# Row selectors of two quads in four moved to GpSimd and ScalarE in the gate scatter of a two-block forward pass

## What is computed

```python
gate = jax.nn.softmax(best, axis=-1)
...
act = jax.nn.gelu(jnp.einsum('tkd,td->tk', u_emb[eb], tb), approximate=False) * gb
return jnp.einsum('tk,tkd->td', act, v_emb[eb])
```

## Time and profile before

| | |
|---|---|
| median of three runs | 1703.91 us |
| the profiled execution, its own time | 1701.01 us |
| its span, first to last instruction | 1699.2 us |
| gate scatter, first selector to last quad | about 920 to 1012 us of the span |
| loop pass of VectorE in the scatter (four quads) | 15 passes, from 927.3 to 1010.5 us |
| granted TensorE clock over the span | 0.99 of full speed |

### The profile page before, as it was taken

How to read it: one execution, slowest core, us unless ns; L and a number is a source line. 1 busy time by engine, 2 the same in 40 slices (tenths; PEclk the granted TensorE clock), 3 DMA queues, 4 the chain that set the end, 5 groups by cost and what they waited for, 6 DMA issues and landing times.

```text
span 1699.2 us, 32624 instructions
## 1 busy us (share of the span) xinstructions
PE 1648.2 (97%) x12606; PEld 1511.1 (89%) x12606; DVE 1174.3 (69%) x2143; ACT 802.4 (47%) x1223; POOL 100.3 (6%) x124
## 2 busy tenths in 40 slices
PE   8999999999999999989999989999999999999998
PEld 3999969999999998879898878999999999999997
DVE  4757746777745779547598998666666666666665
ACT  2524535566535574325214983444444444444444
POOL 0000000022200001200052000000000000000000
PEclk9999999999999999979999999999999999999999
DMA  8866414545554443204233015555555555455553
GB/s 333 311 239 234 165 48 149 189 176 187 179 180 148 149 150 124 77 3 170 103 125 124 26 51 195 178 196 177 193 182 188 190 180 197 175 196 179 191 184 125
DMA packets 38826, 278.94 MB, mean 164 GB/s; under 512 B 4432, under 2 KB 4560, under 8 KB 5328
## 3 DMA queue, kind: packets, MB, share of 16 engines
q1 hardware_dynamic: 35424, 254.82, 41.9%
q0 software_dynamic: 2304, 16.78, 2.6%
q10 hardware_dynamic: 1008, 6.05, 1.0%
HBM read 276.58 MB, written 1.05 MB: 163 GB/s over the span
## 4 chain that ended last, share of the span: by engine, by line
PE 86%; DVE 7%; ACT 4%; issue 2%; DMA 1%; DVEq 0%; POOL 0%; ACTq 0%; POOLq 0%
PE ps L460 86%; DVE piece L1718 2%; ACT piece L1208 1%; DMA ring<-in_stream 1%; DVE pconst_sb L2463 1%; DVE cols L2463 0%; DVE late L2463 0%; DVE arena L1768 0%; DMA small<-in_cT 0%; ACT arena L1247 0%; DVEq L2463 0%; DVE arena L1805 0%; ACT arena L1563 0%; ACT L1243 0%; DVE arena L1785 0%
## 5 line engine op out<-in xcount | busy, mean ns | idle before, releaser
L460 PEld LDWEIGHTS ps<-h_r,piece 128*128 128x128 f32 x5664 | 697.3, 192 | 21.0 <-issue 8.7
L460 PE MATMUL ps<-h_r,piece 128*128 128x256 f32 x5664 | 706.5, 284 | 5.8 <-DVE piece L1718 4.9
L1718 DVE TENSOR_TENSOR piece<-ring,piece 128x1024 fp32r<-128x1024 f32 x434 | 533.3, 1237 | 242.9 <-ACT piece L1208 241.5
L1208 ACT ACTIVATE piece<-ring 128x1024 fp32r<-128x1024 f32 x432 | 452.7, 1056 | 355.1 <-PE ps L460 348.4
L460 PE MATMUL ps<-piece,late_r 128*128 128x512 f32 x1536 | 370.1, 391 | 1.4 <-DVE late_r L2485 1.4
L460 PEld LDWEIGHTS ps<-piece,late_r 128*128 128x128 f32 x1536 | 281.1, 188 | 55.4 <-issue 1.8
L2480 DVE TENSOR_TENSOR late<-late,arena 128x256 f32<-128x256 f32 x113 | 72.1, 638 | 117.5 <-ACT late L1674 117.5
L1674 ACT ACTIVATE late<-ps 128x256 f32<-128x256 f32 x113 | 43.5, 385 | 200.5 <-PE ps L460 200.5
L460 PE MATMUL ps<-arena,ring 128*128 128x256 f32 x480 | 110.5, 379 | 1.6 <-DVE arena L1785 1.6
L460 PEld LDWEIGHTS ps<-arena,ring 128*128 128x128 f32 x480 | 88.1, 190 | 12.3 <-issue 2.0
L460 PE MATMUL ps<-arena 64*64 64x64 f32 (+7 forms) x930 | 90.1, 315 | 9.0 <-DVE arena L2246 3.5
(11 more groups left out here) (325 smaller groups left out, 1703.6 us busy)
## 6 DMA issues: line engine op xcount, KB each, us to landing
ring<-in_stream SPq DMA_DIRECT2D x240, 1024.0 KB, 4.8
arena<-in_mod POOLq DMA_DIRECT2D x16, 1024.0 KB, 6.4
arena<-in_const ACTq DMA_DIRECT2D x1, 2256.0 KB, 10.2
arena<-in_const ACTq DMA_DIRECT2D x1, 1648.0 KB, 9.4
xres<-in_xT SPq DMA_DIRECT2D x1, 1024.0 KB, 6.8
arena<-in_xT SPq DMA_DIRECT2D x1, 1024.0 KB, 7.6
arena<-in_subk ACTq DMA_DIRECT2D x1, 1024.0 KB, 4.9
out<-arena SPq DMA_DIRECT2D x4, 256.0 KB, 2.1
```

The source lines that it names most:

```text
L460: mm_last[0] = nc.tensor.matmul(*args, **kw)
L1208: A(piece[:, 0, c % 3], ring[:, p % RING, s], ACT.Copy).then_inc(S["hi_ready"], 1)
L1718: TT(piece[:, 1, c % 3], ring[:, p % RING, s], piece[:, 0, c % 3].bitcast(F32), ALU.subtract).then_inc(S["lo_ready"], 1)
```

## The change

GpSimd now makes (row - index)^2 for the quads with q mod 4 = 0 and 1: a broadcast subtract and a multiply of the tile by itself, 128x512 each, with a wait on its own semaphore between them. It does so for 32 quads, behind `number` and the two casts in its program. From q = 4 on the subtract waits for the matmuls of quad q - 4. ScalarE clamps these tiles with the same Relu (`rows_end`), and goes on making squares and Relu itself for q mod 4 = 3. VectorE keeps the compare for q mod 4 = 2 only. TensorE waits for `row_hot` in three quads of four. In ScalarE's order the Relu of quads 0 and 1 of each four stands ahead of the copy of quad q - 2. The semaphore `place_no` is renamed `pool_done` and goes on counting (it stands at 35 after `number`).

```diff
--- before.py
+++ after.py
@@ -422,11 +422,11 @@
                 for c in range(2):
                     g.tensor_tensor(e[:, 2 * c:2 * c + 2], e[:, 2 * c:2 * c + 2],
                                     topf[:, :, 2 * hh + c, :].unsqueeze(2).to_broadcast([P, 2, 16, 16]),
-                                    ALU.mult).then_inc(S["place_no"], 1)
+                                    ALU.mult).then_inc(S["pool_done"], 1)
                 steps = 5 * hh + 2
                 for m in (8, 4, 2):
-                    pool.wait_ge(S["place_no"], steps)
-                    g.tensor_tensor(e[:, :, :, 0:m], e[:, :, :, 0:m], e[:, :, :, m:2 * m], ALU.add).then_inc(S["place_no"], 1)
+                    pool.wait_ge(S["pool_done"], steps)
+                    g.tensor_tensor(e[:, :, :, 0:m], e[:, :, :, 0:m], e[:, :, :, m:2 * m], ALU.add).then_inc(S["pool_done"], 1)
                     steps += 1
 
             for hh in range(7):
@@ -439,6 +439,17 @@
                     pool.wait_ge(loaded[first % RING], 16 * (first // RING + 1))
                 pool.wait_ge(S["piece_used"], c - 1 - s)
                 g.tensor_copy(piece[:, 0, c % 3], ring[:, first % RING, s]).then_inc(S["hi_ready"], 1)
+
+            pool.wait_ge(S["selt_sb"], 2)
+            for n in range(L // 8):
+                q = 4 * (n // 2) + n % 2
+                r = row_hot[q % 4]
+                if q >= 4:
+                    pool.wait_ge(S["g_mm"], 2 * q - 6)
+                g.tensor_tensor(r, selT[:, 0, 4 * q:4 * q + 4].unsqueeze(2).to_broadcast([P, 4, P]),
+                                iota.unsqueeze(1).to_broadcast([P, 4, P]), ALU.subtract).then_inc(S["pool_done"], 1)
+                pool.wait_ge(S["pool_done"], 36 + 2 * n)
+                g.tensor_tensor(r, r, r, ALU.mult).then_inc(S["pool_done"], 1)
 
 
         @block.tensor
@@ -1113,8 +1124,8 @@
                 for b in range(2):
                     pe.wait_ge(S["oh_ready"], 2 * q + b + 1)
                     if b == 0:
-                        if q % 2 == 1:
-                            pe.wait_ge(S["row_hot"], q // 2 + 1)
+                        if q % 4 != 2:
+                            pe.wait_ge(S["row_hot"], 3 * (q // 4) + (1, 2, None, 3)[q % 4])
                         if q >= 3:
                             pe.wait_ge(S["g_sb"], q - 2)
                     for e in range(2):
@@ -1645,20 +1656,23 @@
 
             def rows_end(q):
 
-                act.wait_ge(S["row_square"], q // 2 + 1)
+                if q % 4 == 3:
+                    act.wait_ge(S["row_square"], q // 4 + 1)
+                else:
+                    act.wait_ge(S["pool_done"], 37 + 2 * (2 * (q // 4) + q % 4))
                 A(row_hot[q % 4], row_hot[q % 4], ACT.Relu, scale=-1.0, bias=1.0).then_inc(S["row_hot"], 1)
 
             act.wait_ge(S["selt_sb"], 2)
             late_e = CHOICE
             for q in range(L // 4):
-                if q % 2 == 1:
+                if q % 4 == 3:
                     rows(q)
-                if q >= 2 and q % 4 != 1:
+                if q % 4 < 2:
+                    rows_end(q)
+                if q >= 2:
                     gates_out(q - 2)
-                if q % 2 == 1:
+                if q % 4 == 3:
                     rows_end(q)
-                if q >= 2 and q % 4 == 1:
-                    gates_out(q - 2)
                 if late_e < EARLY - 1 and q == 13 + 14 * (late_e - CHOICE):
                     T = TURN["peer"] + late_e
                     act.wait_ge(S["acc_ready"], T + 1)
@@ -2364,7 +2378,7 @@
 
             def gather(hh):
 
-                dve.wait_ge(S["place_no"], 5 * hh + 5)
+                dve.wait_ge(S["pool_done"], 5 * hh + 5)
                 e = place_eq[hh % 2].rearrange("p (c t) k j -> p c t k j", c=2)
                 TT(selv[:, :, 0:2, 16 * hh:16 * hh + 16].rearrange("p t c k -> p c t k"), e[:, :, :, :, 0], e[:, :, :, :, 1],
                    ALU.add).then_inc(S["placed"], 1)
@@ -2456,7 +2470,7 @@
                 for b in range(8):
                     if not (isinstance(i, int) and b < 4):
                         dve.wait_ge(S["g_mm"], 8 * i + (b - 3))
-                    if b % 4 == 0:
+                    if b == 4:
                         TT(row_hot[b // 2], iota.unsqueeze(1).to_broadcast([P, 4, P]),
                            selT[:, 0, bass.ds(16 * i + 2 * b, 4)].unsqueeze(2).to_broadcast([P, 4, P]), ALU.is_equal)
                     for e in range(2):
```

More of the change, by code:

```diff
@@ L98 @@
  decay_exp ffn_ready gelu_done gated gated_hi x_new mqk_pad bon_in w_exp rk_ready const2_in gram_sb
- p1_mm mt_ready places place_no placed hi_ready g_mm selt_sb piece_used acc_ready hn_mm hn_sq hn_sqmm
+ p1_mm mt_ready places pool_done placed hi_ready g_mm selt_sb piece_used acc_ready hn_mm hn_sq hn_sqmm
  xs_sq xs_mm start_sb pconst_in sq1 mod_cols h_ready perm_mm kw_ready state_mm qk_ready probs scores o_sb out_mm
```

## The result

The changed kernel takes 1756.2 us (median of four runs, 1752.2 to 1760.7) against 1703.5 us before (1699.9 to 1703.9): a ratio of 1.032, 95% interval 1.030 to 1.033. The forecast was 1760.4 us. The profiled execution of the changed kernel took 1760.65 us, the slowest of its four; its span is 1758.8 us.

A forecast was written before the change was run, and what follows sets the result against it. VectorE was taken to bound the gate scatter. Its end was summed as 938.6 + 72.5 (15 passes) + 58.8 (60 GpSimd instructions) = 1069.9 against 1010.5, so +59.4 on 1701.01 gives 1760.4 us; range 1742 to 1784.

The forecast's parts named there:

- VectorE is the bound, and one compare less is worth 0.61 us a pass: Gate scatter: runs at VectorE's pace; dropping one compare cuts a pass from 5.44 to 4.83 us, 9 us over 15.
- The late start: Scatter start: GpSimd's selectors stand behind two casts, so quad 1 and all behind it start 11.3 us late.
- the sign "1.26 to 1.8 us": Next profile, if right: GpSimd's TENSOR_TENSORs last 1.26 to 1.8 us, longer where a VectorE compare holds them up.
- The price of one GpSimd instruction to VectorE: Scatter: each GpSimd instruction holds VectorE up by 0.98 us; 60 of them cost 58.8 us.
- The middle between two ends: Price per GpSimd instruction: 0.98 us, between 0.87 (cast scaled by duration) and 1.09 (one column selector let by at each boundary).
- The clock: Rival, scatter: TensorE's waits drop its clock to 1.2 GHz, passes take 9.6 us, total 1773 us; chance 0.14.
- TensorE is not the bound at full clock: Scatter: TensorE needs about 4.6 us a pass, against a forecast pass of 8.75 us.
- No exclusion: Rival, scatter: GpSimd does not hold VectorE up and its own pace decides, 1709.4 us; chance 0.07.
- Full exclusion: Rival, scatter: nothing of VectorE gets through while GpSimd works, 1.35 us per instruction, 1782.6 us; chance 0.12.
- Not slower: Rival: no exclusion and GpSimd instructions of at most 1.21 us with gap, so VectorE decides again, 1701.6 us; chance 0.04.
- The rule of the Trainium skill: Shared SBUF port pair: first issuer blocks the other throughout; 1.27 us for each of 60 instructions, end 17 us later.

The follow-up runs named there:

- `shadow`: The kernel before, with GpSimd making the same 64 instructions into a scratch nobody reads, all other engines keeping their old work: 1757.1 us, ratio 1.032.
- `psum_after`: The changed kernel with the column selectors' tensor input read from a PSUM bank in place of the index constant in SBUF: 1722.9 us.

## Why the prediction was right, and where its terms were off

The direction and the mechanism held, and the measured time lies 4 us under the forecast. Some of that nearness is luck. The forecast was reckoned from an execution of 1701.01 us; by the medians the change costs 52.7 us, 6.7 less than the 59.4, and 2.5 of these are hidden by the low base. More of it lies in errors that cancel. Point by point, for the 54.5 us of the trace against the 59.4 forecast:

- **VectorE is the bound, and one compare less is worth 0.61 us a pass.** Held: 15 x 0.61 = 9 us is all the change could win, and every pass gave it back.
- **The late start** was put at 11.3 us and was 9.9 in the trace; the run without it was 6.3 to 8 us faster, with more collisions. The step that was mis-sized is GpSimd's instruction: I took 1.27 us from the rows of `number`, and the new ones last 1.04, so the sign "1.26 to 1.8 us" did not come either. Same engine, same count of elements, another access pattern; which part of it makes the difference was not tried.
- **The price of one GpSimd instruction to VectorE**, the largest term, was taken as 0.98 us and is 0.78 by the runs with the clock kept up. The form was right (its duration, less one selector that gets by at the boundary: 1.04 - 0.26 = 0.78), and the size was off for the same 1.27. The middle between two ends hid that one of them, with the right duration, is the rule that all these passes follow. Over 60 instructions that is 12 us too much.
- **The clock** was a rival with 0.14 at "9.6 us a pass"; it came in a mild form, as falls to 0.50 for a part of eight passes in fourteen. Mean pass 8.56 against 7.95 with the waits filled: 0.6 x 15 = 9 us in this trace, the slowest of the four (5.9 to 7.7 by the medians), that the forecast's sum lacked. I had argued that TensorE is not the bound at full clock and left it there; but at the moments after GpSimd's burst it was.
- The three errors, -1.4, -12 and +9 us, come to -4.4, against the -4.9 observed. So the sum came closer than its terms did: two sizes were too high and one term was missing, and that they cancel is luck.
- **The other rivals.** No exclusion: refuted by `shadow`, and by `psum_after`, where the same 64 GpSimd instructions ran, no selector was held and the pass fell to 6.27 us. Full exclusion (1.35 us each): refuted, one selector gets by for each instruction. Not slower: the multiply really is faster than the rows of before, at 1.04 us under the 1.21 that it named, but the exclusion that it needed gone is there.
- **The rule of the Trainium skill** ("SBUF — State Buffer", Who interferes with whom), that whoever issues first has the port pair for the whole instruction and the other fully blocks. The trace bears out the block, in both directions. But VectorE loses 0.78 of 1.04 us, since an instruction of its own passes at each boundary; a sum by 1.04 for 60 instructions would be 16 us too high.

No version beats the kernel before: with the start mended and the clock kept up the change is still 40 us behind, because one instruction of GpSimd costs VectorE 0.78 us, and the compare for which GpSimd needs two of them costs 0.61.

## What to carry to other kernels

An idle GpSimd is no free engine beside a VectorE that sets the pace. Here it held both kinds of VectorE instruction in the loop, the compare with two inputs in SBUF and the selector with its tensor in SBUF. Look in the trace for one place where the two engines already overlap, and price a moved instruction by its duration on GpSimd, less the one VectorE instruction that gets by, and not by its cost on VectorE. Ask also what stands ahead of the moved work in the other engine's program; a wait that was free becomes the start of the stage. And where TensorE begins to wait a little in each pass, look at its granted clock, and add the slow moments after the waits to the sum.

## What the runs showed that was not expected

- GpSimd took 1.04 us for these 128x512 float32 operations, 1.27 for those of `number`.
- With one input in PSUM a 128x128 TENSOR_SCALAR costs 0.32 us of pitch instead of 0.257 and is not held by GpSimd at all.
- A GpSimd memset of 0.97 us held VectorE's selectors for some 0.54 us and its compare not at all, 0.38 us on average; a TENSOR_TENSOR of 1.04 us cost 0.78.
- Two waits of TensorE in a pass, one of 1.4 us and one of up to 2.0, went with falls of the clock to 0.50 in eight passes of fourteen; throwaway matmuls in them made the kernel 5.9 to 7.7 us faster.
